# Delta rule: the transposed inverse of each level by four transposes and a ScalarE copy, in place of four products and a VectorE update

## The reference, cut to what matters

```
lmat = jnp.where(strict, jnp.einsum("bhnid,bhnjd->bhnij", k_beta, k) * decay, 0.0)
amat = lmat + jnp.eye(c, dtype=jnp.float32)
rhs = jnp.concatenate([v * beta[..., None], k_beta * jnp.exp(g)[..., None]], axis=-1)
sol = lax.linalg.triangular_solve(amat, rhs, left_side=True, lower=True, unit_diagonal=True)
u, w = sol[..., :dv], sol[..., dv:]
...
v_new = u_i - jnp.einsum("bhcd,bhdv->bhcv", w_i, state)
o_i = jnp.einsum("bhcd,bhdv->bhcv", q_i, state) + jnp.einsum("bhij,bhjv->bhiv", a_i, v_new)
state = state * jnp.exp(gl_i)[..., None, None] + jnp.einsum("bhcd,bhcv->bhdv", k_i, v_new)
```

## Time and profile before

| what | us |
|---|---|
| median of three executions | 2406.88 |
| lowest, highest | 2406.51, 2407.31 |
| the profiled execution, its own time | 2403.88 |
| its span in the trace | 2401.7 |
| the four delta stages of the first layer (262.4 to 526.9) | 264.5 |

### The profile page before, as it was taken

How to read it: one execution, slowest core, us unless ns; L and a number is a source line. 1 busy time by engine, 2 the same in 40 slices (tenths; PEclk the granted TensorE clock), 3 DMA queues, 4 the chain that set the end, 5 groups by cost and what they waited for, 6 DMA issues and landing times.

```text
span 2401.7 us, 40350 instructions
## 1 busy us (share of the span) xinstructions
PE 2319.8 (97%) x15689; PEld 2127.5 (89%) x15689; DVE 1133.3 (47%) x1967; ACT 1113.3 (46%) x1273; POOL 1711.1 (71%) x1340
## 2 busy tenths in 40 slices
PE   8999899999999999998999999999999999999998
PEld 7888889999988888888899999889898888898887
DVE  3334856533333433465665242333524676523776
ACT  4335444446443443454444644335555335555433
POOL 6998545546799899874456568997556997645996
PEclk9999999999999999999999999999999999999999
DMA  7555323234455555542233345555333655323553
GB/s 242 192 192 159 122 89 106 90 104 141 159 192 188 180 189 188 189 153 85 92 102 101 116 146 170 193 191 168 123 106 111 204 186 173 124 98 124 183 192 131
DMA packets 312357, 359.97 MB, mean 150 GB/s; under 512 B 18660, under 2 KB 291104, under 8 KB 312096
## 3 DMA queue, kind: packets, MB, share of 16 engines
q1 hardware_dynamic: 311866, 357.75, 45.8%
q10 hardware_dynamic: 358, 0.33, 0.0%
HBM read 357.01 MB, written 1.05 MB: 149 GB/s over the span
## 4 chain that ended last, share of the span: by engine, by line
PE 85%; DVE 10%; ACT 2%; issue 1%; POOL 1%; DMA 0%; SPq 0%; DVEq 0%; ACTq 0%
PE ps L553 21%; PE ps L753 20%; PE ps L585 17%; PE ps L590 9%; PE ps L632 3%; PE ps L839 1%; PE ps L792 1%; PE ps L648 1%; PE ps L846 1%; POOL sb_lo L526 1%; DVE sb_vT L1865 1%; DVE sb_kT L1865 1%; PE ps L1126 1%; DVE sb_levels L1933 1%; PE ps L848 1%
## 5 line engine op out<-in xcount | busy, mean ns | idle before, releaser
L526 POOL TENSOR_TENSOR sb_lo<-sb_raw,sb_hi 128x512 fp32r<-128x512 f32 (+1 forms) x1336 | 1710.9, 1317 | 672.9 <-ACT sb_hi L1227 671.9
L1227 ACT ACTIVATE sb_hi<-sb_raw 128x2048 fp32r<-128x2048 f32 (+3 forms) x341 | 639.1, 1876 | 654.0 <-PE ps L590 349.2
L585 PE MATMUL ps<-sb_hT,sb_hi 128*128 128x512 f32 x1792 | 426.1, 390 | 0.0
L585 PEld LDWEIGHTS ps<-sb_hT,sb_hi 128*128 128x128 f32 x1792 | 332.7, 188 | 66.7
L753 PE MATMUL ps<-sb_hT,sb_hi 128*128 128x256 f32 x2304 | 311.9, 288 | 6.6 <-DVE sb_hT L1997 2.8
L753 PEld LDWEIGHTS ps<-sb_hT,sb_hi 128*128 128x128 f32 x2304 | 287.5, 192 | 8.1 <-DVE sb_hT L1997 3.2
L590 PEld LDWEIGHTS ps<-sb_hT,sb_lo 128*128 128x128 f32 x1792 | 229.8, 191 | 8.7
L1785 DVE TENSOR_TENSOR sb_yinv<-ps,sb_row 128x512 f32<-128x512 f32 x112 | 77.5, 692 | 335.0 <-PE ps L590 334.9
L590 PE MATMUL ps<-sb_hT,sb_lo 128*128 128x256 f32 x1792 | 232.4, 283 | 0.0
L553 PE MATMUL ps<-sb_hi,sb_o_h 128*128 128x512 f32 x560 | 219.6, 392 | 0.9 <-DVE sb_o_l L1792 0.9
L553 PE MATMUL ps<-sb_hi,sb_o_l 128*128 128x512 f32 x560 | 218.6, 390 | 0.0
(11 more groups left out here) (385 smaller groups left out, 3731.4 us busy)
## 6 DMA issues: line engine op xcount, KB each, us to landing
sb_raw<-in_ffn_w_in SPq DMA_DIRECT2D x88, 1024.0 KB, 5.1
sb_raw<-in_w_in SPq DMA_DIRECT2D x78, 1024.0 KB, 5.2
sb_raw<-in_ffn_w_out SPq DMA_DIRECT2D x44, 1024.0 KB, 4.9
sb_raw<-in_ffn_w_up SPq DMA_DIRECT2D x44, 1024.0 KB, 5.1
sb_raw<-in_ffn_w_down SPq DMA_DIRECT2D x22, 1024.0 KB, 4.8
sb_raw<-in_w_out SPq DMA_DIRECT2D x16, 1024.0 KB, 5.1
sb_raw<-in_w_branch_a SPq DMA_DIRECT2D x8, 1024.0 KB, 5.1
sb_raw<-in_w_branch_b SPq DMA_DIRECT2D x8, 1024.0 KB, 5.0
```

Source lines behind the costliest of these rows:

```text
L526: ins = nc.gpsimd.tensor_tensor(lo[:, slot, c], raw[:, slot, c], hi[:, slot, c].bitcast(F32), ALU.subtract)
L585: mm(ps[:, bank + i, :].rearrange("p (h n) -> p h n", h=2), wh[:, c, i * P:(i + 1) * P], hT_both[:, :, c, :], start=c == 0, stop=False, sk ...
L1227: fn(hi[:, slot, 0:width], raw[:, slot, 0:width], ACT.Copy).then_inc(hi_ready, 1)
```

## The change

For all levels but the last, the four products of L848 go, and with them DVE's update of `xinv`. A new step r comes behind q: it waits for DVE's update of `yinv`, transposes the four blocks of `yinv` into bank 5 (L852 in the numbering of the changed kernel), and ACT copies bank 5 to `xinv` (L1378). The next p waits for that copy. A stage has 26 steps where it had 22, `DELTA_WEIGHT` gets four more ones, and the same number of parts is spread over them.

```diff
-DELTA_WEIGHT = [2, 3, 2] + [1] * 10 + [1.3, 1, 1, 1, 1, 1, 1, 1.5, 2]
+DELTA_WEIGHT = [2, 3, 2] + [1] * 14 + [1.3, 1, 1, 1, 1, 1, 1, 1.5, 2]
...
@@ PE
                     if i == 0:
                         wa("x")
                     else:
-                        wv(f"x{i - 1}")
+                        wa(f"x{i - 1}")
...
                     for p in range(4):
                         ins = mm(blk(2, p), of(plev, p), of(yinv, p), start=True, stop=True)
-                        if i < LEVELS - 1:
-                            ins = mm(blk(5, p), of(yinv, p), of(plev, p), start=True, stop=True)
                     ins.then_inc(dl_pe, 1)
                     yield
+                    if i < LEVELS - 1:
+                        wv(f"y{i}")
+                        for p in range(4):
+                            ins = nc.tensor.transpose(blk(5, p), of(yinv, p), ident)
+                        ins.then_inc(dl_pe, 1)
+                        yield
@@ ACT
                     fn(plev[:], ps[:, 3, :], ACT.Copy).then_inc(dl_act, 1)
                     yield
                     yield
+                    if i + 1 < LEVELS:
+                        wp(f"r{i}")
+                        fn(xinv[:], ps[:, 5, :], ACT.Copy).then_inc(dl_act, 1)
+                        yield
@@ DVE
                     wp(f"q{i}")
-                    if i + 1 < LEVELS:
-                        tt(xinv[:], xinv[:], ps[:, 5, :], ALU.subtract).then_inc(dl_dve, 1)
                     tt(yinv[:], yinv[:], ps[:, 2, :], ALU.subtract).then_inc(dl_dve, 1)
                     yield
+                    if i + 1 < LEVELS:
+                        yield
```

More of the change, by code:

```diff
@@ L145 @@
 LEVELS = 5
-DELTA_PE = Steps(["rows", "eg", "gram", "tok", "xt"] + [f"{a}{i}" for i in range(LEVELS) for a in "pq"]
+DELTA_PE = Steps(["rows", "eg", "gram", "tok", "xt"] + [f"{a}{i}" for i in range(LEVELS) for a in ("pqr" if i + 1 < LEVELS else "pq")]
                  + ["uw", "kv0", "ws1", "kv1", "ws2", "kv2", "ws3", "o", "osum"])
@@ L149 @@
 HALVES = 2 * NPAIR
-DELTA_ACT = Steps(["decay", "x"] + [f"p{i}" for i in range(LEVELS)] + ["uw", "osq", "ors"])
+DELTA_ACT = Steps(["decay", "x"] + sum([[f"p{i}"] + ([f"x{i}"] if i + 1 < LEVELS else []) for i in range(LEVELS)], []) + ["uw", "osq", "ors"])
 DELTA_DVE = Steps(["diff", "lt", "m0"]
-                  + sum([[f"m{i + 1}" if i + 1 < LEVELS else "tok"] + ([f"x{i}"] if i + 1 < LEVELS else []) + [f"y{i}"]
+                  + sum([[f"m{i + 1}" if i + 1 < LEVELS else "tok"] + [f"y{i}"]
                          for i in range(LEVELS)], [])
```

## The result

The changed kernel takes 2419.43 us (median of five executions, 2417.40 to 2421.06) against 2406.51 us for the kernel before (five, 2404.19 to 2407.31): a ratio of 1.0056, 95% interval 1.0042 to 1.0069. It is slower by 12.9 us. The profiled execution of after has 2419.43 us and a span of 2417.6 us, 15.9 us above the span of before.

The account below looks back on a forecast made before the run. The prediction took PE's own work and waits as the bound (PE busy 97% of the span). Waits +14.5 and work -8.2 gave +6.3 us a layer, +12.6 in all: 2419.5 us, range 2411 to 2429.

Parts of the forecast that it names:

- The work saved: PE's work in each level but the last: 0.51 us less a level, 8.2 us a layer.
- (a): PE's waits for the first `yinv` ahead of the first transposes (L829): 5.7 us a layer.
- (b): Empty filler slots with nothing else in DVE's or ACT's queue: waits of 10.6 us a layer.
- (c): Step r waiting for the update of `yinv` behind half a convolution: 11.2 us a layer, bounds 9.1 to 14.0.
- The worked case: Level 0's step r in stage 2: PE waits 2.85 us for the update of `yinv`, 1.28 before.
- (d): The scan's empty slots, ws1 in all four stages and ws3 in stage 2: waits of 3.7 us a layer.
- The clock: Granted clock in the delta stages: one fall a layer as before; none would be 3.4 us less in all.
- Stage 4: The fourth delta stage: 2.1 us longer than before.
- three signs of being wrong: Stage 4 not longer, p waiting for ACT behind filled slots too, or (c) outside 8 to 13 us.
- The slots cover the third round trip: Rival: PE finds every `xinv` and `yinv` ready, only the saving stays, 2390.5 us; 4 in 100.
- DVE's relief: Rival: fewer DVE updates ahead of `yinv` shorten (c), no clock falls, 2407 to 2411 us; 9 in 100.

Follow-up runs that it names:

- e2: The changed kernel with each group of four transposes issued twice; 2435.17 us, ratio 1.0128 to the kernel before.
- e7: The changed kernel with products in stages 1 and 2 (22 steps), filler parts placed, convolution halves held behind the update of `yinv`; 2381.20 us.
- e9: e7 with products in all stages, same parts at the same places, an empty step r in stages 3 and 4; 2387.09 us.
- e3: The changed kernel with convolution halves not queued at a level's step p but at the next step, behind the update of `yinv`; 2401.70 us.
- e4: The changed kernel with the filler parts placed by hand, one behind every step r of stages 3 and 4, none at kv2; 2412.37 us.
- e10: e7 with transposes and 26 steps in all four stages, parts, halves held; 2384.74 us.
- e11: The changed kernel with the copy of bank 5 to `xinv` done by DVE in place of ACT; 2433.24 us.
- e1: The kernel before, products kept, with the changed kernel's 26-step plan and an empty step r; 2398.74 us, ratio 0.9977.
- e5: The kernel before (products, 22 steps) with convolution halves held behind the update of `yinv`; 2410.02 us, ratio 1.0026.

## Why the prediction was right, point by point

**The bound.** Right, as far as the runs test it: the time goes by PE's work and PE's waits. e2 put 0.43 us on the path for each group of transposes added.

**The work saved.** Right in the mechanism, a little high: 0.51 us a level forecast, 0.46 measured where it is covered (e7 against e9). The Trainium skill's rule (TensorE: Matmul & The Clock Gate, section Terms), a transpose mode four times faster for FP32, would have given 0.67 as an estimate. No run here agrees with it: four transposes take 0.39 to 0.43 us from start to start against 0.90 for four products, 2.1 to 2.3 times faster.

**(a) L829.** 5.7 forecast, 4.8 measured. Stages 1 to 3 came as forecast (1.5, 1.2, 1.05), the fourth at 1.05 in place of 1.85: L1931, 1.66 us as in the earlier trace rows, started 0.8 us earlier against PE.

**(b) Empty slots.** 10.6 forecast; measured 5 x 0.99 (p behind an empty r), 0.88 (p1 in stage 2) and 5 x 0.97 (q4, q3 and q2): 10.7.

**(c) The update behind half a convolution.** 11.2 forecast, 10.2 measured, inside its bounds: 1.02 and 2.43 in stage 1; 2.33, 1.03 and 0.54 in stage 2; 2.11 and 0.54 in stage 3; 0.17 in stage 4. The worked case, r0 in stage 2, was 2.85 and came at 2.33, and r0 in stage 3 came higher than I had it (its mask product took 1.78 us), r1 lower (0.69 us, where I had counted a slow one). So the term came out in the lower half of its bounds, and not in the upper half, as I had read the rule of the port pair to give. My uncertain term was the mask product, which ran quicker more often, with a median of 694 ns for L1941 of after where the earlier trace rows has 1214:

```profile
L1941 DVE TENSOR_TENSOR sb_levels<-sb_levels,sb_const x32: 691/694/1781, 274.4 to 1321.1; 128x512 f32<-128x512 f32 x32
```

e3 shows the term by taking the cause away: L852's waits fall from 12.1 to 4.5 us a layer, and 1.9 of what is left belongs to (b). Of the 16.6 us that e3 gains a part is the clock (see there), so they are more than this term.

**(d) The scan.** 3.7 forecast; 4 x 0.71 and 0.7 measured, 3.5.

**The sum.** Waits of 29.1 us in place of 31.2. But a wait costs more than its entry: from the transposes at 487.61 to p at 489.06 are 1.45 us, which is 0.39 + 1.06 where the row says 0.99. Some 0.08 us for each of the 13 waits more is 1.0 us a layer. So 29.1 + 1.0 - 16.7 - 8.2 = +5.2 us a layer at full clock, against +6.3 forecast. The traces have +3.8 for the first layer's stages (262.75 to 266.54 us), and +5.5 once the fall of the clock is counted that before has in it, 1.7 us, and after has not.

**The clock.** This is the part that I had right by balance only. I kept one fall a layer. In the delta stages of after's first layer there is none. In those of the second there are three, two in stage 1 and one in stage 3, each 3.4 us at half the clock, at instructions that kept the full clock in the first layer. Windows of after, the first layer and then the second (PE, PEld, DVE, ACT, POOL busy, granted clock, DMA):

```profile
280.00:290.00 10.00, 8.79 (x72) 8.42 (x72) 7.34 (x18) 3.78 (x5) 1.82 (x2) 1.00 0.33 105
290.00:300.00 10.00, 7.08 (x59) 6.89 (x60) 4.16 (x9) 1.80 (x4) 4.97 (x4) 1.00 0.34 107
...
1100.00:1110.00 10.00, 9.08 (x63) 8.90 (x64) 5.65 (x14) 2.20 (x4) 1.62 (x2) 0.83 0.34 105
1110.00:1120.00 10.00, 7.76 (x55) 7.57 (x54) 4.80 (x12) 2.59 (x3) 4.96 (x4) 0.83 0.24 69
```

The second layer's stages took 271.07 us, 4.5 us more than the first's, with the same waits (11.9, 4.9, 4.8, 2.9, 2.8). So of the 15.9 us that the span grew, 12.1 lie in the delta stages (3.8 and 8.3), where I had 12.6. Another 0.3 us lie ahead of the first stage, and 3.4 us in what follows the second layer's stages, where I had nothing and where the change touches no instruction. It isn't the clock: both kernels have two falls there, each 0.72 over 6 us, and one at the very end. PE's waits for DVE and ACT in the layers of the second kind are longer in after: 5.0 us at L1014, where L1010 of before has 3.7, and 2.6 us at L610 where before has 0.8, so 3.1 us. Summed over all that follows the second layer's delta stages, PEld waits 46.4 to 47.8 us in the profiles of the six kernels in which ACT copies the transposes (after, e2, e3, e4, e7, e10), and 43.7 to 44.5 us in those of the seven others. e11, with the transposes and DVE's copy, is among these (44.4 us, and 1.5 us at L610 as before). So the longer waits go with ACT's copies and not with the transposes; how the edit reaches that far stays open. On the medians the growth is 12.9 us. That the median came out as forecast to 0.1 us is luck; what was forecast well is the waits, term by term.

**Stage 4.** 2.1 us longer forecast, 1.9 measured. That is partly balance: L829 waited 0.8 us less than forecast, and the wait of 0.17 us at r0, the smaller saving of a level and what each wait costs beyond its entry took most of it back. p waited for ACT behind empty r slots only. With (c) at 10.2 us, none of the three signs of being wrong that the prediction names came true.

**The rivals.** "The slots cover the third round trip" did not happen, but e7 shows that it can: with a part at every r slot and the halves held, stages 3 and 4 have no wait at L875 and the kernel is 22.5 us faster than before. Against it I had said that no product can be moved into the wait; the parts could be. "DVE's relief" came in part: the mask products were quicker (median 694 ns for 1214) and no clock fell in the first layer, but (c) was 10.2 us and not 9.1, the clock fell in the second layer, and the time is 8 us above that rival's. No run takes the update of `xinv` away by itself: e1, which keeps it, is 19.5 us faster than the change, but differs in the form as well.

What I did not see at all is that the new plan alone is a gain of 6.6 us. I booked the empty slots as a loss of the change (a, b and d, 20 us a layer), and did not ask what the same slots do for products: their p waits fell from 9.7 to 2.6 us a layer.

## What to carry to other kernels

Trading work on the bound engine for one more round trip pays where filler stands behind every leg of the trip (0.46 us a level here) and costs about 1 us at each leg without one; so lay the filler first, and choose the form by stage. What is queued on the answering engine ahead of the answer counts as much as the answer: 1.96 us of convolution in front of a 0.68 us update made 6.1 us of waits a layer, and 16.6 us in all with the falls of the clock that the run without it did not have. Holding it back too far held up the projections instead. One profile is one execution: look at the granted clock of the others before explaining a median by its waits (e4). When an edit changes a plan (where the filler stands) as well as a form (how a result is computed), time the plan alone.

## What the runs showed of the hardware

- **The mask product and GpSimd.** L1933 of before and L1941 of after, 16 in the first layer of each: the 13 during which no POOL instruction ran took 0.69 us, each of them; 17 of the 19 others took 0.87 to 1.80 us, the remaining two 0.69. One of the long ones of after (1.44 us), with what POOL did:

```profile
337.96 5.44 POOL L526 TENSOR_TENSOR sb_lo<-sb_raw,sb_hi 128x512 fp32r<-128x512 f32 x4 [0.38 <-ACT sb_hi L1231]
```

  It covers 338.36 to 339.80. The Trainium skill (Trainium Architecture — The Big Picture, section What this means for kernel authors) says that VectorE and GpSimd share a port pair under an exclusive lock; these rows agree with it, for this operation, whose inputs are both in SBUF. Over both layers of both kernels the ends tell more: 34 mask products began while an instruction of L526 ran, and 33 of them ended 0.55 us (545 to 551 ns) after that instruction did, whether they had then taken 0.87 or 1.80 us. The other one began 0.05 us before its end and took 0.69. The three that began first, 0.14 to 0.15 us ahead of an instruction of L526, took 0.69 us as well. So the length follows the end of the POOL instruction that is running when the product begins. No run here took POOL's work away, so the price is read from times and not from an experiment.
- **The clock.** The same instructions with nearly the same waits (12.1 and 11.9 us at L852) kept the full clock in the first layer of after and lost it in the second (above). After the wait of 3.52 us in e5 the granted clock was at the 1.2 GHz level, and the next twelve weight loads took 2.63 us where they take 1.50 at full clock. A fall cannot be assigned to a wait of this kernel from its length alone: after kept its clock behind 2.43 and 2.33 us in the first layer, before lost it behind 2.91. What decides it stays open.
- **DVE's copy from PSUM** of 128x512 takes 0.68 to 0.69 us, as its subtraction from there does; the same copy on ACT 0.60.
